# First attention of a two-block transformer kernel: heads taken in pairs, probabilities normalised before they are turned, V as the stationary operand

## The reference, cut to what matters

```
s = q @ k.T * 64**-0.5 + mask          # 128 x S, S = 128 (qt + 1)
p = exp(s - max(s)) / sum(exp(s - max(s)))
o = p @ v                              # 128 x 64
out_nsa = g0 * o_cmp + g1 * o_1 + g2 * o_2
```

## Time and profile before

| | |
|---|---|
| median of 3 runs | 4474.55 us (4472.01 to 4479.48) |
| span of the profiled execution | 4370.0 us |
| median less span | 104.6 us |
| PE busy | 3684.3 us (84%) |
| DVE busy | 2180.5 us (50%) |
| ACT busy | 846.3 us (19%) |
| first attention, from its first scores to the output projection | 293.3 to 675.2 us, 381.9 us |

### The profile page before, as it was taken

One profiled execution on the slowest core, in us unless ns is written; L12 is line 12 of the kernel. 1 busy time (PEld: TensorE's weight loads), 2 busy tenths in 40 slices (PEclk: granted clock), 3 DMA queues, 4 the chain that ended last, 5 costly groups with the idle time before them and its releaser, 6 DMA issues.

```text
span 4370.0 us, 33503 instructions
## 1 busy us (share of the span) xinstructions
PE 3684.3 (84%) x10958; PEld 1877.5 (43%) x10958; DVE 2180.5 (50%) x4839; ACT 846.3 (19%) x1788; POOL 1195.4 (27%) x1151
## 2 busy tenths in 40 slices
PE   8788899899999799993999997476877678788787
PEld 4345564444445356542654456333433233233222
DVE  0547532310001356895652544885478778544443
ACT  1223321200003222113211122201122122111111
POOL 0200000000000000000000101335377777777775
PEclk9875758999999998995999998788999899999999
DMA  3340011122221111320122235677499999999998
GB/s 152 140 146 1 14 45 39 52 76 75 77 96 58 53 58 53 104 79 29 45 80 76 80 119 192 218 243 273 176 406 368 352 365 385 368 408 409 368 406 320
DMA packets 171916, 765.20 MB, mean 175 GB/s; under 512 B 19256, under 2 KB 19256, under 8 KB 160224
## 3 DMA queue, kind: packets, MB, share of 16 engines
q0 software_dynamic: 157904, 580.06, 35.2%
q1 hardware_dynamic: 13824, 182.97, 11.5%
q10 hardware_dynamic: 16, 0.02, 0.0%
HBM read 744.08 MB, written 18.89 MB: 175 GB/s over the span
## 4 chain that ended last, share of the span: by engine, by line
PE 49%; DVE 20%; POOL 9%; DMA 8%; issue 6%; ACT 3%; POOLq 0%; DVEq 0%; ACTq 0%
PE ps L252 13%; PE ps L258 9%; POOL arena L2589 8%; DMA arena<-in_pu,arena 5%; PE ps L1278 5%; PE ps L1336 5%; DVE arena L2619 5%; DVE arena L1422 4%; PE ps L2542 3%; PE ps L220 3%; PE ps L814 2%; PE ps L1560 2%; PE ps L832 2%; DMA arena<-in_pv,arena 2%; PE ps L1547 1%
## 5 line engine op out<-in xcount | busy, mean ns | idle before, releaser
L2542 PE MATMUL ps<-arena 128*128 128x512 f32 x2048 | 1001.8, 631 | 320.5 <-DMA arena<-in_pv,arena 159.3
L2619 DVE CUSTOM_DVE_ANT_0 arena<-arena 128x1024 f32<-128x1024 f32 x512 | 623.5, 1221 | 377.8 <-DMA arena<-in_pu,arena 376.7
L252 PE MATMUL ps<-arena 128*128 128x512 f32 (+1 forms) x1768 | 759.8, 590 | 31.4 <-ACT arena L2108 24.4
L2542 PEld LDWEIGHTS ps<-arena 128*128 128x128 f32 x2048 | 379.0, 197 | 925.4 <-issue 518.1
L2589 POOL DMA_INDIRECT arena<-in_pu,arena x512 | 540.6, 1056 | 372.3 <-issue 82.8
L2589 POOL DMA_INDIRECT arena<-in_pv,arena x512 | 545.4, 1065 | 193.3 <-issue 107.3
L258 PE MATMUL ps<-arena 128*128 128x512 f32 (+2 forms) x1408 | 527.1, 536 | 3.1 <-DVE arena L1251 0.9
L252 PEld LDWEIGHTS ps<-arena 128*128 128x128 f32 x1768 | 339.0, 193 | 437.4 <-issue 432.2
L220 PE MATMUL ps<-arena 128*128 128x128 f32 (+1 forms) x1094 | 218.1, 339 | 212.6 <-ACT arena L858 70.5
L258 PEld LDWEIGHTS ps<-arena 128*128 128x128 f32 x1408 | 267.8, 190 | 261.8 <-issue 219.4
L263 POOL TENSOR_TENSOR arena<-arena 128x1 f32<-128x1 f32 (+7 forms) x38 | 61.1, 1610 | 1106.8 <-DVE arena L675 396.7
(11 more groups left out here) (328 smaller groups left out, 3037.5 us busy)
## 6 DMA issues: line engine op xcount, KB each, us to landing
arena<-in_w_in SPq DMA_DIRECT2D x27, 2048.0 KB, 8.2
arena<-in_w_ada SPq DMA_DIRECT2D x12, 2048.0 KB, 8.1
arena<-in_w_ff_in SPq DMA_DIRECT2D x8, 2048.0 KB, 7.8
arena<-in_w_ff_out SPq DMA_DIRECT2D x8, 2048.0 KB, 8.0
arena<-in_w_pq SPq DMA_DIRECT2D x8, 2048.0 KB, 8.7
aside<-arena POOLq DMA_DIRECT2D x20, 512.0 KB, 5.9
arena<-in_w_at SPq DMA_DIRECT2D x4, 2048.0 KB, 8.0
arena<-in_w_o SPq DMA_DIRECT2D x4, 2048.0 KB, 8.2
```

What stands on the lines that cost most here:

```text
L252: x = t.matmul(PS[:, b, 0:n], hT[:, k, i * 128:(i + 1) * 128], w[:, k, :], start=k == 0, stop=k == nk - 1)
L2542: x = t.matmul(PS[:, b + c, :], DG[n % 4], row(f)[:, 512 * c:512 * c + 512], start=j == 0, stop=j == 127)
L2619: v.tensor_tensor_reduce(row(f), row(f), TT[i], 1.0, 0.0, ALU.mult, ALU.add, DOT[i % 2][:, j:j + 1]).then_inc(*pe.V.step("dot", 128 * i + j))
```

## The change

The units become 48 groups `(qt, p, br)`: one pair `p` of neighbouring heads and one branch. An iteration now handles two heads.

- PE: both heads' scores stand directly behind one another, in banks (0, 1, 2) in turn. The probabilities are turned in one bank, 3, head by head. V (128 x 64) is now the stationary operand and 128 columns of turned probabilities stream; head h writes PSUM partitions 64h to 64h+63, so the result is already turned. Branch 0 fills the first 128 columns of a bank of (4, 5); the compressed branch, branch 1 and branch 2 add up in the next 128.
- DVE: the probabilities are scaled in the store by gate / sum before they are turned (`scaled`), S columns for each head. Negated maximum, reciprocal and gate are done for two heads at once. The compressed branch is scaled before it is turned (`cp`).
- ACT: the same copies and exponentials, in the order copy, exponential, copy, exponential; one copy per three groups from PSUM to `OT`.
- `after_tensor`, `after_scalar` and `O1` are gone, and with them the scaled sums on DVE.
- `attn_hook` runs three steps per group, and `memory_*` starts at group 23 with one step per group.

```diff
-            b = bank(t, (6, 7), at1.V, "co", qt)
-            t.wait_ge(*at1.A.at("pc", qt))
-            for g in range(2):
-                x = t.matmul(PS[:, b, 256 * g:256 * g + 256], PC[:, g, :], BV[:, g, :], start=True, stop=True)
-            x.then_inc(*at1.P.step("co", qt))
...
+            at1.V.own(v).tensor_tensor(s3, s3, bc(SM[:, 16:24], 32), ALU.mult).then_inc(*at1.V.step("cp", qt))
...
-                if j >= 44:
+                if j >= 23:
                     drain(memory, 1)
                 if n < 3:
-                    drain(coming[n], 1 + r % 3 // 2 if r < 23 else 100)
+                    drain(coming[n], 3 if r < 11 else 100)
...
+            for j in range(NG + 3):
+                if j < NG:
...
+                    for h in range(2):
+                        bank(t, (0, 1, 2), at1.V, "free", j, h)
+                    for h in range(2):
+                        t.matmul(PS[:, held(at1.V, "free", j, h), 0:S], T[64 * h:64 * h + 64, (0 if br == 0 else 8) + p, qs], keys(br, p, h)[:, 0:S],
+                                 start=True, stop=True).then_inc(*at1.P.step("s", j, h))
+                for h in range(2):
+                    if 0 <= j - 2 < NG:
...
+                        t.wait_ge(*at1.V.at("scaled", i, h))
+                        b = bank(t, (3,), at1.A, "pt", i, h)
+                        for a in range(GROUPS[i][0] + 1):
+                            y = turned(t, PS[:, b, 128 * a:128 * a + 128], x[:, 128 * a:128 * a + 128])
+                        y.then_inc(*at1.P.step("t", i, h))
+                    if 0 <= j - 3 < NG:
...
+                        if h == 0 and br == 1:
+                            t.wait_ge(*at1.A.at("pc", qt))
+                            t.matmul(PS[:, b, o], BV[:, p // 2, 128 * (p % 2):128 * (p % 2) + 128], PCS[qt % 2][:, p // 2, :],
+                                     start=True, stop=False).then_inc(*at1.P.step("cv", qt, p))
+                        t.wait_ge(*at1.A.at("pt", i, h))
+                        for a in range(qt + 1):
+                            y = t.matmul(PS[64 * h:64 * h + 64, b, o], values(br, p, a), turned_probs(i, h)[:, 128 * a:128 * a + 128],
+                                         start=br == 0 and a == 0, stop=br != 1 and a == qt)
+                        y.then_inc(*at1.P.step("pv", i, h))
+                hook(j)
...
+                    for h in range(2):
+                        v.wait_ge(*at1.P.at("s", j, h))
+                        v.tensor_tensor_reduce(probs(j, h), PS[:, held(at1.V, "free", j, h), 0:S], m, 1.0, -3.0e38, ALU.add, ALU.max, r[:, h:h + 1]
+                                               ).then_inc(*at1.V.step("free", j, h))
+                    at1.V.own(v).tensor_scalar(r[:, 2:4], r[:, 0:2], -SCALE, None, ALU.mult).then_inc(*at1.V.step("neg", j))
+                if j > 0:
...
+                    for h in range(2):
+                        v.tensor_scalar(probs(i, h), probs(i, h), r[:, 6 + h:7 + h], None, ALU.mult).then_inc(*at1.V.step("scaled", i, h))
```

More of the change, by code:

```diff
@@ L696, in build @@
         MKS = [take(512) for _ in range(2)]
[L697 to L700, removed]
+        SBG = [PJ[:, j, 0:1024] for j in range(4)]
+        PTG = [take(1024) for _ in range(3)]
+        RWG = [take(8) for _ in range(4)]
         CSC = take(256)
-        PC = take(256).rearrange("p (g n) -> p g n", g=2)
+        PCS = [take(256).rearrange("p (g n) -> p g n", g=2) for _ in range(2)]
         SM = take(32)
@@ L1013, in before_vector @@
-            yield
-            yield
[L1016 to L1029, removed]
@@ L1056, in build, with keys, values @@
-        place(at1, units1, SB1, PT1)
-        def attn_hook(coming, memory, after):
+        GROUPS = []
+        for qt in range(4):
+            for p in range(4):
+                for br in range(3):
+                    GROUPS.append((qt, p, br))
+        NG = len(GROUPS)
+        def keys(br, p, h):
+            return T[64 * h:64 * h + 64, (12, 14 + p // 2, 16 + p // 2)[br], :]
+        def values(br, p, a):
+            o = (1352, 1608)[br - 1] + 64 * (p // 2)
+            return VD[:, a, :] if br == 0 else PJ[:, a, o:o + 64]
@@ L1059, in f, with result, probs, turned_probs @@
+        def result(qt, p, br):
+            n, o = 4 * qt + p, 128 * (br > 0)
+            return n, 4 + n % 2, slice(o, o + 128)
+        def probs(j, h):
+            S = 128 * (GROUPS[j][0] + 1)
+            return SBG[j % 4][:, S * h:S * h + S]
+        def turned_probs(j, h):
+            S = 128 * (GROUPS[j][0] + 1)
+            return PTG[j % 3][:, S * h:S * h + S]
+        def attn_hook(coming, memory):
             def f(j):
-                n, r = divmod(j, 24)
-                if r == 3 and n:
-                    after(n - 1)
@@ L1072, in attn_tensor @@
             memory = memory_tensor(t)
-            soft_tensor(t, at1, units1, 2, attn_hook([before_tensor(t, q) for q in (1, 2, 3)], memory, lambda q: after_tensor(t, q)))
+            hook = attn_hook([before_tensor(t, q) for q in (1, 2, 3)], memory)
+            for j in range(NG + 3):
+                if j < NG:
+                    qt, p, br = GROUPS[j]
+                    S, qs = 128 * (qt + 1), slice(128 * qt, 128 * qt + 128)
+                    for h in range(2):
[5 more added lines that the diff above has]
+                    if 0 <= j - 2 < NG:
+                        i = j - 2
+                        x = probs(i, h)
+                        t.wait_ge(*at1.V.at("scaled", i, h))
[4 more added lines that the diff above has]
+                    if 0 <= j - 3 < NG:
+                        i = j - 3
+                        qt, p, br = GROUPS[i]
+                        n, b, o = result(qt, p, br)
+                        if h == 0 and br == 0:
+                            bank(t, (4, 5), at1.A, "oc", n)
+                        if h == 0 and br == 1:
[8 more added lines that the diff above has]
+                hook(j)
```

89 lines of the change are left out of this document (49 added, 40 removed).

## The result

The changed kernel takes 4359.56 us (median, 4348.94 to 4376.23) against 4473.28 us of the kernel before on the same chip: ratio 0.9756, interval [0.9729, 0.9783], 114 us less. Forecast were 4391 us and -83 us. The range 4350 to 4430 holds the time, the forecast's own range 4372 to 4410 does not: the gain is more than a third larger than forecast.

A forecast was written before the change was run, and what follows sets the result against it. Bound by DVE in the first tile, DVE and PE in the second, PE at 1.2 GHz in the fourth; tiles -5, -9, -38, -29 (together -81), output projection -2: -83, forecast 4391 us, own range 4372 to 4410.

The forecast's parts named there:

- The limit of each tile: First attention before the change: first tile DVE's, second half DVE's and half PE's, fourth PE's, busy 120.1 of 121.2 us.
- Scores of two heads as one head's: PE's scores: two heads overlap and cost 2.00 us for S = 512 at half clock, saving 2.00 per group.
- Full clock in the fourth tile: Fourth tile begins at full clock, since the dense products stand behind its first four groups, 36 to 39.
- A group of the fourth tile at 3.9 us, taken as 4.0: PE at full clock: scores 1.06, transposes 1.0, 16 passes 1.76, compressed product 0.1; 12 groups at 4.0 make 48 us.
- the 3 us for a first group at half clock: Fourth tile: 3 us added because its first group runs partly at half clock.
- the head norm: Fourth tile: four steps of 1.2 us on DVE where it has 0.6 to spare, +3 us.
- The tiles bound by DVE: 56, 69 and 84 us: First three query tiles of the attention: forecast gains of 5, 9 and 38 us, 28 of the last from moved dense products.
- A group of DVE: Search parts of the first three tiles: 5.3 groups each at 2.2, 2.6 and 3.0 us, besides the search rounds.
- The three indexer groups: First three tiles: groups with indexer steps, three per tile, at 4.5, 6.0 and 7 us each.
- Rival 1: Attention: DVE's parts run at DVE's sum, PE keeps full clock, 50 + 61 + 75 + 88 = 274; 4365 us, chance 0.16.
- Nothing gained in later stages but 2 us: Behind the attention: same instructions in both kernels; only the output projection gains, beginning at full clock, -2 us.
- `w_out` hidden by nothing to spare, at worst +3: End of the stage: the panel load needs about 8 us beside an 8.5 us tail; at worst +3.

The follow-up runs named there:

- the moved memory steps: Kernel before, with memory steps from unit 60 instead of 44, putting the dense products at the fourth tile's start: ratio 0.9918, attention 336.9 us.
- the second profile: The changed kernel run again with no edit: ratio 0.9777, attention 282.6 us.
- scores apart: Changed kernel, with the second head's scores issued behind the first head's transposes and product: ratio 0.9872, attention 336.9 us.

## Why the prediction was right, and where it was off

The direction, the stage and most of the mechanism were right. Of the 33 us by which the stages' -116 exceeds the forecast's -83, 21 are the tiles' and 10 the scan stage's. That the fourth tile came out within 4 us is in part luck, and the other three were costed too high.

- *The limit of each tile.* Right in part: PE in the fourth tile, DVE in the searches, by the windows and by the run without scaling. The groups ahead of and behind the search are not DVE's; in the second tile that is half of the time.
- *Scores of two heads as one head's.* Right: 1.06 us for four passes of 512 columns, 1.91 when both use one half. The Trainium skill's rule of strict program order ("TensorE: Matmul & The Clock Gate", "Part 3: Packing small matmuls") would have given three pass times, by estimate some 1.5 us; the trace disagrees again.
- *Full clock in the fourth tile.* The outcome was right, the ground was not. The prediction has the tile begin at full clock because the dense products stand at its start. In the old order they do raise it, by the moved memory steps; in the changed kernel the clock had risen 13 us ahead of them, and it rose without them in the run with the memory steps at group 14.
- *A group of the fourth tile at 3.9 us, taken as 4.0.* Mis-sized: 4.29. The passes are 0.11 us apart as costed. Missing were the changes of form, for which the full-clock sum had little: eight product passes take 1.03 us rather than 0.88, four transposes 0.58 rather than 0.5. With 0.11 us for each pass, 0.14 to 0.15 us are left for each change. The tile still came out 3 us under its 92, since the 3 us for a first group at half clock and the 3 us for the head norm did not come: PEclk was 1.00 throughout, and PE's only idle time, 0.7 us, is the wait for `w_out`. These errors cancel.
- *The tiles bound by DVE: 56, 69 and 84 us.* Measured are 50.4, 66.9 and 73.6 (76.8 in the second profile). This was mis-sized most, in two terms. A group of DVE was charged 2.2, 2.6 and 3.0 us beside its search rounds; groups with three rounds are 4.6, 5.8 and 7.0 us apart, rounds 0.99, 1.25 and 1.52, which leaves 1.6, 2.0 and 2.4. DVE goes through the small steps of a group (0.47 us from L1130 to L1142, not 0.65) and on into the scaling and the search without waiting, here in the first tile:

```profile
318.50 0.17 DVE L1130 TENSOR_SCALAR arena<-arena 128x2 f32<-128x2 f32 x1
318.97 0.48 DVE L1142 TENSOR_SCALAR arena<-arena 128x128 f32<-128x128 f32 x2
319.49 0.43 DVE L977 MAX8 arena<-arena 128x8 f32<-128x256 f32 x1
320.48 0.43 DVE L977 MAX8 arena<-arena 128x8 f32<-128x256 f32 x1
```

  The three indexer groups, charged 13.5, 18 and 21 us because their steps go round three engines, took 11.2, 18.9 and 16.4: too much in the first and third tile, right in the second.
- *Rival 1, DVE's own sum, 4365 in all.* Closer to the time than the forecast, but not right throughout: its 50, 75 and 88 us fit the first, third and fourth tile, its 61 us for the second are 6 short, and a total so near owes something to the 10 us of the next point, which neither had.
- *Nothing gained in later stages but 2 us.* Wrong by 10 us: the scan stage's code is unchanged, yet took 875.2 us instead of 885.1. Both stand at 512 us into the stage alike; the next 116 us, here as windows of the kernel before and of the changed one, differ in the clock:

```profile
1969.30:2085.40 116.10, 41.22 (x150) 32.23 (x151) 65.91 (x122) 45.20 (x47) 0.00 (x0) 0.50 0.05 19
```
```profile
1862.70:1978.80 116.10, 41.01 (x196) 30.37 (x197) 70.72 (x129) 47.69 (x50) 0.00 (x0) 0.62 0.06 21
```

  The second got through 196 instead of 150 passes. In the twelve profiles this stage took 872 to 885 us. Its start does not explain that: with the memory steps moved in the kernel before, the stage started at 1411.4 us and took 882.1; with scores apart it started at 1410.8 us and took 872.4. What decides when the clock rises there stays open.
- *`w_out` hidden by nothing to spare, at worst +3.* Right within that: the panel took the 8.2 us forecast as about 8, and PE waited 0.71 us.

## What to carry to other kernels

Before costing a rewrite of a stage, read PE's granted clock in it and try the cheapest move that puts dense products at its start: here one number gave 45 us in the old order. Where an engine bounds a stretch and the others run ahead of it, its own sum is the estimate for that stretch, and for no more than it. Small products on different halves of the array run together if they are neighbours, by row halves as one head behind the other, by column halves in full only pass by pass in turn; the changes of form between them are worth counting.

## What the runs showed of the hardware

- Of three orders, products on different column halves overlap in full only when they alternate: 16 passes took 2.06 us apart, 1.53 as eight and eight, 1.03 alternating.
- A change between 64-row, 128 x 128 and 64-column form costs about 0.14 us at 2.4 GHz, worked out from blocks of passes 0.11 us apart (1.03 us for eight, 0.58 for four). Between the transposes and the product of the kernel before, which share a form, hardly anything is lost: 0.84 us for eight passes in the rows of the moved memory steps.
- PE can be busy in every window and stay at 1.2 GHz: the fourth tile before, and 74.5 of 77.2 us in the second tile with scores apart. With both heads' scores in a row it got 2.4 GHz with no dense product near, 13 us ahead of the first one and, in another run, 29 us behind the last.
- The kernel before took 4369 us on one chip and 4473 us on another. The changed kernel's two profiles, 4347 and 4265 us long on two chips, place such a difference: the DMA gather stage took 1752.9 and 1665.7 us, all the rest together differs by 5 us.
